# State-space parameters loaded in the projection, a new order of u, y and mem steps, and one transfer for row two of the down product

## The reference

```python
h = rmsnorm(x, g_mix)
u, q, k, v = split(h @ w_in)                       # 512 columns each
# head group A: 32 groups of 16 channels, each drives a diagonal complex state of 64
a_bar = exp((a_re + 1j * a_im) * exp(log_dt)); b_bar = (a_bar - 1) / lam * b
states = scan(s -> a_bar * s + b_bar @ u)          # over the 2048 positions
y_ssm  = gated(gelu(real(c @ states) + d * u))
# head group B: stick-breaking attention over q, k, v, 8 heads of 64
x = x + concat(rmsnorm(y_ssm), rmsnorm(y_sb)) @ w_out
x = x + cross_attention(rmsnorm(x), rmsnorm(mem))  # 4 heads over 256 memory tokens
x = x + relu(rmsnorm(x) @ w_up) ** 2 @ w_down      # inner width 4096
```

## Time and profile before

| | us |
|---|---|
| median of three runs | 3012.65 |
| profiled execution | 3006.3 |
| its span, first to last instruction | 3004.5 |
| PE busy | 2803.8 (93%) |
| DVE busy | 1913.6 (64%) |
| ACT busy | 1357.6 (45%) |
| POOL busy | 936.6 (31%) |

### The profile page before, as it was taken

The page is one execution under the profiler, slowest core; times in us unless marked ns, Lnnn a source line. Parts: engine busy times, 40 slices in busy tenths (PEclk is TensorE's granted clock), DMA queues, the critical chain, the costliest instruction groups (busy, mean ns, idle before and its releaser), DMA issues. The chain is left out here.

```text
span 3004.5 us, 43240 instructions
## 1 busy us (share of the span) xinstructions
PE 2803.8 (93%) x14883; PEld 2367.3 (79%) x14883; DVE 1913.6 (64%) x2803; ACT 1357.6 (45%) x2268; POOL 936.6 (31%) x743
## 2 busy tenths in 40 slices
PE   6999967879999998997899989999999999999999
PEld 5888854669899897886788778887888787878777
DVE  5334338768778786545667675657555868686864
ACT  4222224657667675322344455556555424242321
POOL 0011100745455552320000032333323344444443
PEclk9999988989999999998999999999999999999999
DMA  5333345263422203344132334333544374756555
GB/s 169 92 87 81 99 125 71 55 189 72 95 57 57 61 22 102 105 147 161 36 119 105 117 104 136 103 108 130 179 139 140 102 167 100 170 95 154 119 111 88
DMA packets 296004, 328.21 MB, mean 109 GB/s; under 512 B 114584, under 2 KB 221088, under 8 KB 295584
## 3 DMA queue, kind: packets, MB, share of 16 engines
q1 hardware_dynamic: 276960, 291.96, 32.7%
q0 software_dynamic: 18432, 33.56, 7.9%
q10 hardware_dynamic: 464, 0.79, 0.1%
HBM read 206.57 MB, written 126.88 MB: 111 GB/s over the span
## 5 line engine op out<-in xcount | busy, mean ns | idle before, releaser
L3235 PE MATMUL f_ps_bank<-f_big,h_wv 128*128 128x512 f32 x1280 | 503.1, 393 | 25.6 <-DVE f_big L3081 20.3
L3236 PE MATMUL f_ps_bank<-f_big,h_wv 128*128 128x512 f32 x1280 | 500.0, 391 | 0.0
L3237 PE MATMUL f_ps_bank<-f_big,h_wv 128*128 128x512 f32 x1280 | 500.0, 391 | 0.0
L704 POOL TENSOR_TENSOR a_w<-a_on,a_left 128x640 f32<-128x640 f32 (+5 forms) x192 | 282.1, 1469 | 243.3 <-DVE a_left L756 108.9
L3077 DVE TENSOR_TENSOR h_wv<-h_w_raw,h_wv 128x512 fp32r<-128x512 f32 x189 | 241.9, 1280 | 155.1 <-ACT h_wv L2978 151.7
L2978 ACT ACTIVATE h_wv<-h_w_sum 128x512 fp32r<-128x512 f32 x252 | 158.9, 631 | 349.7 <-PE f_ps_bank L3237 342.2
L2919 POOL TENSOR_TENSOR h_w_sum<-h_w_raw 128x512 f32<-128x512 f32 x63 | 91.2, 1447 | 721.6 <-DMA h_w_raw<-in_w_up 441.8
L3235 PEld LDWEIGHTS f_ps_bank<-f_big,h_wv 128*128 128x128 f32 x1280 | 241.5, 189 | 83.5 <-issue 28.8
L3237 PEld LDWEIGHTS f_ps_bank<-f_big,h_wv 128*128 128x128 f32 x1280 | 241.4, 189 | 50.7
L3236 PEld LDWEIGHTS f_ps_bank<-f_big,h_wv 128*128 128x128 f32 x1280 | 241.7, 189 | 49.5
L846 PE MATMUL a_ps_y<-a_wt,a_v 128*96 128x128 f32 x2176 | 269.9, 273 | 3.3 <-DVE a_yt L779 3.3
(11 more groups left out here) (400 smaller groups left out, 6211.2 us busy)
## 6 DMA issues: line engine op xcount, KB each, us to landing
h_w_raw<-in_w_up SPq DMA_DIRECT2D x32, 1024.0 KB, 6.7
a<-h_xr SPq DMA_DIRECT2D x128, 256.0 KB, 3.4
h_w_raw<-a SPq DMA_DIRECT2D x32, 1024.0 KB, 5.1
out<-h_xr POOLq DMA_DIRECT2D x128, 256.0 KB, 4.0
h_raw<-in_w_down SPq DMA_DIRECT2D x32, 512.0 KB, 6.5
p_xt<-in_x SPq DMA_DIRECT2D x16, 512.0 KB, 4.5
p_raw<-in_w_in SPq DMA_DIRECT2D x16, 512.0 KB, 5.4
q<-p_raw SPq DMA_DIRECT2D x64, 128.0 KB, 2.5
```

The source lines that it names most:

```text
L704: pool.tensor_tensor(w[m % WS][:, 0:k1 - k0], on[m % ONS][:, 0:k1 - k0], left[a][i % 2][:, at + k0 + 1:at + k1 + 1], ALU.mult).then_inc(we ...
L3235: pe.matmul(o, wv(i, 0)[:, k, :], hv(i, 0)[:, k, :], start=(k == 0), stop=False)
L3236: pe.matmul(o, wv(i, 0)[:, k, :], hv(i, 1)[:, k, :], start=False, stop=False)
L3237: mm = pe.matmul(o, wv(i, 1)[:, k, :], hv(i, 0)[:, k, :], start=False, stop=(k == KH - 1))
```

## The change

In the projection: a class `ScanInputs` holds the parameters' tiles in a tensor `spare`, which also gives two of the four raw weight tiles; SP issues the twelve loads in the third step (`c == 2`), when the weights are split, and waits for them at the end of the projection.

In the state-space stage: the twelve loads are gone from SP's program. Slab 0 of u is loaded when the memory is turned, slab 1 when the values are made, slab 2 as before behind the stores of keys and values. DVE makes the memory's reciprocal root behind the angles instead of first. ACT makes the sines behind the scaling of the memory instead of behind the copies of the turned memory. In the loop ACT copies y of pair p - 1 between the two table parts of pair p + 3 instead of behind both.

In the down product: R21 and R22 change places, so that row two lies in one piece of 4 KB per partition, and `grow_out` sends it once, when C22 is made, instead of in two transfers behind C21 and C22. `GROWN` lets both tiles wait for that transfer.

```diff
--- before.py
+++ after.py
+class ScanInputs:
...
+        self.params_in = sem("params_in")
+        flat = spare[:, :, :].rearrange("p a f -> p (a f)")
+        self.b_in = flat[:, 0:2 * G * C].rearrange("p (x g c) -> p x g c", x=2, c=C)
+        self.c_rows = flat[:, 2 * G * C:2 * G * C + 12 * PC].rearrange("p (s x q) -> p s x q", s=4, x=3)
+        self.a_rows = flat[0:G, 2 * G * C + 12 * PC:2 * G * C + 16 * PC].rearrange("p (x y q) -> p x y q", x=2, y=2)
+        self.dt = small[:, 3 * P:3 * P + G]
+
+    def load(self, sp):
+        for part, src in enumerate(self.a):
+            for copy in range(2):
+                sp.dma_start(self.a_rows[:, part, copy, :], src).then_inc(self.params_in, DMA)
+        sp.dma_start(self.dt, self.log_dt.partition_broadcast(P)).then_inc(self.params_in, DMA)
+        for h in range(2):
+            for x in range(2):
+                sp.dma_start(self.b_in[h * self.PC:(h + 1) * self.PC, x, :, :], self.b[h ^ x].rearrange("g p c -> p g c")
+                             ).then_inc(self.params_in, DMA)
+        for part, src in enumerate((self.c[0], self.c[1], self.c[0])):
+            sp.dma_start(self.c_rows[:, :, part, :], src.rearrange("(s g) c p -> (g c) s p", s=4)).then_inc(self.params_in, DMA)
+
+
...
-        w_raw = [raw[:, i, :] for i in range(4)]
+        raw = sb("raw", [P, 2, 1024])
+
+        w_raw = [raw[:, 0, :], raw[:, 1, :], spare[:, 0, :], spare[:, 1, :]]
...
@@ -222,6 +252,9 @@
             def body(c, b, more):
                 if more:
                     load_x(c + 1)
+                if c == 2:
+                    sp.wait_ge(w_split, W_PIECES)
+                    scan.load(sp)
...
             for c in range(STEPS):
                 body(c, c % 2, c < STEPS - 1)
+            sp.wait_ge(scan.params_in, scan.LOADS * DMA)
...
@@ -999,16 +1030,6 @@
         def _(sp):
             for j in range(MT):
                 sp.dma_start(mt[:, j, :], mem[j * P:(j + 1) * P, :]).then_inc(mem_in, DMA)
-            for part_, src in ((0, a_re), (1, a_im)):
-                for copy in range(2):
-                    sp.dma_start(a_rows[:, part_, copy, :], src).then_inc(params_in, DMA)
-            sp.dma_start(dt[:, :], log_dt.partition_broadcast(P)).then_inc(params_in, DMA)
-            for h, parts in ((0, (b_re, b_im)), (1, (b_im, b_re))):
-                for x in range(2):
-                    sp.dma_start(b_in[h * PC:(h + 1) * PC, x, :, :], parts[x].rearrange("g p c -> p g c")
-                                 ).then_inc(params_in, DMA)
-            for part_, src in enumerate((c_re, c_im, c_re)):
-                sp.dma_start(c_rows[:, :, part_, :], src.rearrange("(s g) c p -> (g c) s p", s=4)).then_inc(params_in, DMA)
             def load_u(slab):
...
+            sp.wait_ge(mem_turned, MT)
+            load_u(0)
+            sp.wait_ge(values_made, MT)
+            load_u(1)
             sp.wait_ge(kv_copied, 4)
             sp.dma_start(kt_dram, kt).then_inc(kv_stored, DMA)
             sp.dma_start(mv_dram, mv).then_inc(kv_stored, DMA)
             sp.wait_ge(kv_stored, 2 * DMA)
-            for slab in range(US):
-                load_u(slab)
+            load_u(2)
...
@@ -1108,6 +1132,9 @@
             act.wait_ge(mem_scaled, 1)
             for j in range(MT):
                 act.activation(mt[:, j, :], mt[:, j, :], ACT.Copy, scale=mstat[:, 2, j:j + 1]).then_inc(mem_normed, 1)
+            act.wait_ge(angles, 1)
+            act.activation(num[:, 6, :], num[:, 5, :], ACT.Sin).then_inc(sines, 1)
+            act.activation(num[:, 7, :], num[:, 5, :], ACT.Sin, scale=0.5).then_inc(sines, 1)
             act.wait_ge(gm_turned, 1)
...
-            act.wait_ge(angles, 1)
-            act.activation(num[:, 6, :], num[:, 5, :], ACT.Sin).then_inc(sines, 1)
-            act.activation(num[:, 7, :], num[:, 5, :], ACT.Sin, scale=0.5).then_inc(sines, 1)
...
             for p in range(1, PAIRS):
                 if p + 3 < PAIRS:
                     parts(p + 3, 0)
+                copy_y(p - 1)
+                if p + 3 < PAIRS:
                     parts(p + 3, 1)
-                copy_y(p - 1)
             copy_y(PAIRS - 1)
...
-            dve.wait_ge(mem_squared, MT)
-            rsqrt_mean(dve, link, mstat[:, 0, :], D_MODEL, mstat[:, 1, :], mstat[:, 2, :], mstat[:, 3, :])
-            dve.sem_inc(mem_scaled, 1)
             dve.wait_ge(params_in, 12 * DMA)
...
             dve.tensor_scalar(num[:, 5, :], r_, -3.1415925, 3.1415925, ALU.max, ALU.min).then_inc(angles, 1)
+            dve.wait_ge(mem_squared, MT)
+            rsqrt_mean(dve, link, mstat[:, 0, :], D_MODEL, mstat[:, 1, :], mstat[:, 2, :], mstat[:, 3, :])
+            dve.sem_inc(mem_scaled, 1)
             tt(x_, lam[:, 0, :], step, ALU.mult)
             exp_of(e_, x_, k_, r_)
             tt(rho[:, :], e_, e_, ALU.mult)
...
         def r_tile(i):
-            return xr[:, 2 + i // 2, i % 2 * BANK:(i % 2 + 1) * BANK]
+            half = (0, 1, 1, 0)[i]
+            return xr[:, 2 + i // 2, half * BANK:(half + 1) * BANK]
...
-        grown = [sem(f"grown{i}") for i in range(4)]
+        grown = [sem(f"grown{i}") for i in range(3)]
+        GROWN = [grown[i] for i in (0, 1, 2, 2)]
...
-            def grow_out(b, made_by, i, row, half):
+            def grow_out(b, made_by, i, row, half, src, width):
                 t = (b - ALL) % DOWN_BLOCKS * 2 + row
                 if b == ALL:
                     pool.wait_ge(x2_copied, SEQ // P * DMA)
                 pool.wait_ge(combined.sem, combined.at(b, made_by))
-                pool.dma_start(out[t * P:(t + 1) * P, half * BANK:(half + 1) * BANK], r_tile(i),
-                               accum_op=ALU.add).then_inc(grown[i], DMA)
+                pool.dma_start(out[t * P:(t + 1) * P, half * BANK:half * BANK + width], src,
+                               accum_op=ALU.add).then_inc(GROWN[i], DMA)
             for b in range(1, END + 2):
                 if b < END:
                     sum_one(b)
-                if b - 2 >= ALL:
-                    grow_out(b - 2, C21, 3, 1, 0)
                 if b < END:
                     sum_two(b)
                 if b - 2 >= ALL:
-                    grow_out(b - 2, C22, 2, 1, 1)
+                    grow_out(b - 2, C22, 2, 1, 0, xr[:, 3, :], D_MODEL)
                 if b < END:
                     sum_three(b)
                 if b - 2 >= ALL:
-                    grow_out(b - 2, C12, 1, 0, 1)
+                    grow_out(b - 2, C12, 1, 0, 1, r_tile(1), BANK)
                 if b < END:
                     sum_four(b)
                 if ALL <= b - 1 < END:
-                    grow_out(b - 1, C11, 0, 0, 0)
+                    grow_out(b - 1, C11, 0, 0, 0, r_tile(0), BANK)
         @block.scalar
         def _(act):
@@ -3114,7 +3139,7 @@
                 if not down:
                     dve.wait_ge(stored[i].sem, stored[i].at(b - 1, DMA))
                 elif plain or b > ALL:
-                    dve.wait_ge(grown[i], (b - ALL) * DMA)
+                    dve.wait_ge(GROWN[i], (b - ALL) * DMA)
```

28 lines of the change are left out of this document (16 added, 12 removed).

## The result

| | executions | median, us | lowest to highest |
|---|---|---|---|
| before | 4 | 3015.35 | 3012.24 to 3018.19 |
| after | 4 | 2989.14 | 2985.60 to 2991.22 |

After divided by before is 0.9919, with a 95% interval from 0.9907 to 0.9930: 24 us less, between 21 and 28. The forecast was 2997.4 us, 15.2 less than 3012.65, and its range ended at 2991. So the direction held and the size did not. The profiled executions differ by 3006.3 - 2990.3 = 16.0 us only, which looks like the forecast. Most of what follows is about that contradiction, and about two terms of the sum that were off in opposite directions.

The account below looks back on a forecast made before the run. TensorE was taken to bound the down product without a gap, two meeting routes the state-space start, and waits for GpSimd the pair loop. -11.1 - 5.0 + 0.9 = -15.2 us: 3012.65 to 2997.4 us, range 2991 to 3006.

Parts of the forecast that it names:

- Parameters early, projection free: Twelve parameter loads issued in the projection: TensorE starts 12.7 us earlier in the state-space stage, at no cost in the projection.
- Order of VectorE and ScalarE: State-space start: memory's root behind the angles leaves VectorE 10.2 us ahead; sines end 0.3 us before VectorE needs them.
- The seam: Start of the state-space stage up to ScalarE's first table copy: two routes meet, tables start at 508.2 instead of 519.33, -11.1 us.
- low table ready: 518.0 - 10.2: End of VectorE's chain ahead of the tables: 518.0 moved 10.2 us earlier, to 507.8.
- ScalarE's route: TensorE and ScalarE's path over memory, keys, transposes, kernel and crossed products to the tables: ready at 508.2.
- The loop: Loop over 16 pairs: y copied in ScalarE's wait, turn 5.15 to 4.65 us, ten turns, -5.0 us.
- The rival in which GpSimd and VectorE fill the gap: Pair loop stays as long because GpSimd's operations meet VectorE's on shared ports: -10.2 us in all, 3002.4 us; chance 0.19.
- that of a low clock in the kernel products: TensorE's clock stays low in the state-space kernel products, route 7.2 us later: gain 8.0, 3004.6 us; chance 0.08.
- at the three inner chunk boundaries ... 0 to -2 us there; I take 0: Down product, where VectorE is late for TensorE: fewer GpSimd issues could give 0 to -2 us; taken as 0.
- the tail: Kernel end: the last transfer stands behind a row-two transfer twice as long, +0.9 us, bounds 0 and +1.9.
- The slower rival: Down product: row-two transfer holds VectorE's tile write in every block, 2 us in each of 31, +62, 3059 us; chance 0.05.
- case of more than forecast: Both state-space routes shorten fully and TensorE alone sets the pair loop: -12.7 - 6.8 = -19.5, 2993.2 us; chance 0.10.

## Why the prediction was right or wrong

**Parameters early, projection free: right.** The twelve are issued from 133.4 to 143.3 us, 9.9 us of SyncE's time, behind the next step's x. The state-space stage starts at 420.2 after and 420.1 to 421.8 before.

**Order of VectorE and ScalarE: right.** The root takes its 2.4 us behind the angles, and the sines are 0.44 us early.

**The seam: the step "low table ready: 518.0 - 10.2" was right by its rows and short by what was in them.** The table copy comes 84.52 us behind the stage start in place of 97.53: -13.0, against -11.1 forecast and the bound of 12.7. Of the missing 1.9 us, 0.4 are ScalarE's route, which the sum took as the later one. The rest is the copy held by the clearing, 2.01 us before and 0.43 after. The line stood in the timeline of before with almost five times the duration that the same copy has elsewhere, and it was moved along as if it were work. A further 1.8 us appear only against other traces of before: its seam is 97.5, 98.2, 100.4 and 101.3 us (mean 99.3) in the four traces where this part is unchanged, so that the gain is 14.8. The ScalarE route was ready by 504.72 - 2.30 = 502.4, 82.2 us behind the stage start, where 508.2 - 421.8 = 86.4 was forecast: too slow by 4, which cost nothing as it no longer binds. Part of the 4 is TensorE's clock: the first v products took 5.3 us in place of 6.6, at a granted clock of 0.77 and then 0.64 in place of 0.50 and 0.55, behind a wait of 1.43 us in place of 7.16.

**The loop: right.** -4.7 by the traces, -6.3 (3.3 to 9.3) timed, -5.0 forecast. The rival in which GpSimd and VectorE fill the gap falls, as does that of a low clock in the kernel products: 64 products in the 7.1 us from 487.27 to 494.36 are the length that they had.

**Row two in one transfer: wrong in two terms of the sum.** The first is "at the three inner chunk boundaries ... 0 to -2 us there; I take 0": it is -5.3. The bound had no row behind it. In the block ahead of a boundary, where VectorE is behind, what is taken off VectorE comes back nearly whole (1.9 us off the subtraction, 1.8 off the distance), and nothing in the prediction asked what GpSimd's issue does to VectorE. The row with 3.49 us for a subtraction that takes 0.69 in the changed kernel stood in the trace of before. The second is the tail, +0.9 with bounds 0 and +1.9: its mechanism, a longer transfer in front of the last, is worth 0.3 us, but the end of the kernel is 3.4 longer, for a cause outside of it: GpSimd's drain, which ends 3.2 us later behind the transfers and which no step of the prediction had. The slower rival (VectorE held by the long transfer) falls: VectorE waits 10.0 us in all for these transfers, and TensorE does not feel it.

**The base: wrong.** Profiled execution and median were taken as shifted by a constant 6.3 us. The shift held for neither kernel: the second profiled execution of before (3016.11) and the one of after (2990.34) lie above the medians of their runs (3014.35 and 2989.14). Two of the four traces of before in which this part is unchanged have the stall of 3.4 us in the state-space stage, and the change takes it away; that it is also part of what the median of the timed runs has more is likely but not shown, as only traces tell the stages.

**The sum, corrected**: -14.8 (seam, mean of traces) - 4.7 - 5.1 + 3.4 = -21.2 us, where the timed runs have -23 (19 to 27) and -24 (21 to 28). With the down product alone, -6.0 in place of -5.1, it is -22.1. What remains lies inside the intervals. Three small slips in the prediction's own sums change nothing of this: the keys' transposes come 4.02 + 1.4 = 5.4 us earlier by its rows and not 5.3, y is there at 561.97 + 2.85 = 564.8 and not 564.9, and its case of more than forecast leaves out the 0.9 of the tail.

## What to carry to other kernels

Before moving a chain of operations, read the durations in it: an operation that takes several times what its size needs is a collision, and a shift in time changes it. Count an issue on GpSimd as time in which its next operation is pushed on, and look at which VectorE operation it is pushed onto, above all in blocks where VectorE is late already. Take two traces of the kernel before when its timed runs lie on one side of the profiled one; the stage in which they differ is a term of the sum.

## What the runs showed that was not expected

- A MEMSET of 3.51 us on GpSimd held a VectorE operation on eight columns for 3.58 us (0.17 otherwise) and left products of two tensors of 4096 columns at 4.42.
- A software DMA issue of 2 KB per block costs as much as one of 256 KB: 5.1 us over 32 blocks (2996.31 against 2991.17), by the traces 8.0 more in the MLP and 3.4 less at the end. What it changes is where GpSimd's sums meet VectorE's subtractions.
- GpSimd's DRAIN ahead of the last barrier took 4.8 us with four issues in each down block and 8.2 with three, whatever the last blocks did, and the barrier waited for it. The view of waits named another engine.
- A 256 KB accumulating transfer landed in 4.0 us with four a block and in 4.7 when one of three in a block was 512 KB, which took 5.6.
